# Modulation products kept whole on four column strips, and first squares added in pairs, in a decoder layer with product-key experts

## What is computed

```python
mod = silu(c) @ w_ada + b_ada        # c: 9 conditioning vectors of 1024, w_ada 1024 x 6144
sh1, sc1, gt1, sh2, sc2, gt2 = split(mod, 6)
h = rms_norm(x, g_pre1) * (1 + sc1) + sh1
P = h @ w_in                         # 3584 columns: q, k, v, g, and B, C, xv of a short convolution
m = concat(retention(q, k, v, g), short_conv(B, C, xv)) @ w_out
x = x + gt1 * rms_norm(m, g_post1)
h = rms_norm(x, g_pre2) * (1 + sc2) + sh2
x = x + gt2 * rms_norm(peer(h), g_post2)
```

## Time and profile before

| | us |
|---|---|
| median of 3 runs | 1785.98 (1785.57 to 1786.85) |
| the profiled execution | 1788.07 |
| its span, first to last instruction | 1786.3 |
| PE busy | 1737.2 (97%) |
| VectorE busy | 1095.5 (61%) |
| ScalarE busy | 587.0 (33%) |
| GpSimd busy | 1052.1 (59%) |
| mean granted TensorE clock | 0.991 of full |

### The profile page before, as it was taken

The page is one execution under the profiler, slowest core; times in us unless marked ns, Lnnn a source line. Parts: engine busy times, 40 slices in busy tenths (PEclk is TensorE's granted clock), DMA queues, the critical chain, the costliest instruction groups (busy, mean ns, idle before and its releaser), DMA issues.

```text
span 1786.3 us, 31229 instructions
## 1 busy us (share of the span) xinstructions
PE 1737.2 (97%) x12724; PEld 1695.1 (95%) x12724; DVE 1095.5 (61%) x2204; ACT 587.0 (33%) x764; POOL 1052.1 (59%) x693
## 2 busy tenths in 40 slices
PE   7989999999999999999999999999999999999996
PEld 5989979699999999999999999999999999999996
DVE  5624586567477456667562222225888989888884
ACT  5222264332233323232222222223333333333332
POOL 0330100006687888888888888873667787767631
PEclk9999999999999999999999999999999999999997
DMA  8523399673466665666657666668999999999971
GB/s 327 189 83 120 122 363 322 216 233 83 99 130 134 139 126 125 143 126 126 143 119 146 139 142 142 132 138 313 363 354 358 362 364 370 367 366 376 380 295 48
DMA packets 192358, 385.18 MB, mean 216 GB/s; under 512 B 74376, under 2 KB 132104, under 8 KB 177368
## 3 DMA queue, kind: packets, MB, share of 16 engines
q1 hardware_dynamic: 111864, 306.56, 50.5%
q0 software_dynamic: 80352, 76.65, 19.7%
HBM read 318.44 MB, written 64.19 MB: 214 GB/s over the span
## 4 chain that ended last, share of the span: by engine, by line
PE 51%; DVE 10%; issue 7%; POOL 3%; DMA 2%; ACT 0%; DVEq 0%; SPq 0%; ACTq 0%
PE ps L1672 27%; PE ps L1692 23%; DVE ul L1862 2%; DMA qp<-vtab,packed_choice 2%; POOL qp L1826 2%; POOL ag L1819 1%; DVE topi L135 1%; DVE top L129 1%; DVE topi L125 0%; PE ps L1649 0%; DVE h L214 0%; DVE h L223 0%; DVE h L228 0%; DVE pick L218 0%; DVE pick L235 0%
## 5 line engine op out<-in xcount | busy, mean ns | idle before, releaser
L100 POOL DMA_INDIRECT gates_dram<-gate,where x384 | 646.6, 1684 | 271.0 <-DVE where L251 130.9
L1672 PE MATMUL ps<-hl,uh 128*128 128x260 f32 x2048 | 414.3, 283 | 7.6 <-DVE ul L1862 7.6
L1672 PE MATMUL ps<-hh,ul 128*128 128x260 f32 x2048 | 414.0, 284 | 0.0
L1672 PE MATMUL ps<-hh,uh 128*128 128x260 f32 x2048 | 413.4, 284 | 0.0
L1862 DVE TENSOR_TENSOR ul<-us,uh 128x1024 fp32r<-128x1024 f32 x132 | 161.0, 1223 | 365.0 <-issue 280.4
L1692 PE MATMUL ps<-cl,uh 128*128 128x384 f32 (+1 forms) x1024 | 345.2, 337 | 3.2 <-DVE ul L1862 1.8
L1692 PE MATMUL ps<-ch,ul 128*128 128x384 f32 x1024 | 344.1, 336 | 0.0
L1692 PE MATMUL ps<-ch,uh 128*128 128x384 f32 x1024 | 344.1, 336 | 0.0
L1672 PEld LDWEIGHTS ps<-hl,uh 128*128 128x128 f32 x2048 | 317.0, 189 | 8.8 <-DVE ul L1862 8.6
L1672 PEld LDWEIGHTS ps<-hh,ul 128*128 128x128 f32 x2048 | 317.0, 189 | 0.0
L1672 PEld LDWEIGHTS ps<-hh,uh 128*128 128x128 f32 x2048 | 316.2, 189 | 0.0
(11 more groups left out here) (245 smaller groups left out, 2240.6 us busy)
## 6 DMA issues: line engine op xcount, KB each, us to landing
us<-utab SPq DMA_DIRECT2D x128, 512.0 KB
pairs<-vtab SPq DMA_DIRECT2D x62, 1024.0 KB
gates_dram<-blank SPq DMA_DIRECT2D x24, 1024.0 KB, 9.7
ahead_dram<-a SPq DMA_DIRECT2D x128, 192.0 KB
qp<-ahead_dram SPq DMA_DIRECT2D x32, 768.0 KB
gt<-gates_dram SPq DMA_DIRECT2D x32, 768.0 KB
wr<-w_ada SPq DMA_DIRECT2D x21, 1024.0 KB, 7.7
wr<-w_in SPq DMA_DIRECT2D x13, 1024.0 KB, 4.8
```

Source lines behind the costliest of these rows:

```text
L100: nc.gpsimd.indirect_dma_start(out=io["gates"].rearrange("g p c a t -> (g p c a t)").unsqueeze(1), out_offset=bass.IndirectOffsetOnAxis(ap ...
L1672: last = nc.tensor.matmul(out[:, half, :], w, r[:, k, half * TH:(half + 1) * TH], start=(k == 0 and q == 0), stop=(k == KD - 1 and q == 2))
```

## The change

Every modulation product is whole. `cs` is padded to 32 columns with zeros; the eight k-tiles go in turn to four column strips, that is to output partitions 0 to 31, 32 to 63, 64 to 95 and 96 to 127 of one PSUM bank, two k-tiles accumulating on each. ScalarE copies all 128 partitions, and the turn multiplies by `pick_row`, which adds the four partial rows. The split loads of w_ada, `cp`, `both` and the extra split buffers are gone, with their `high` and `low` calls in the start and in the heads. The first w_in load stands third in the order, no longer sixth. PE makes four products before the first blocks (product and turn three times, then a product) and the others ahead of k = 1 to 4. The squares of the first norm are added in pairs on VectorE, so that PE sums four tiles and not eight. The 24 clearing writes stand two behind each of the loads 11 to 22 (the projections), no longer behind the last 24.

The diff, cut to its core (buffers and semaphores that only vanish are left out):

```diff
@@ -52,6 +52,8 @@
+STRIP = 32
+STRIPS = P // STRIP
@@ -59,7 +61,7 @@
-    order = [(ADA, at) for at in shift_and_scale[:5]] + [(WIN, 0)] + [(ADA, at) for at in shift_and_scale[5:]]
+    order = [(ADA, at) for at in shift_and_scale[:2]] + [(WIN, 0)] + [(ADA, at) for at in shift_and_scale[2:]]
@@ -351,10 +349,10 @@
-        cs = sb(stack, "cs", [P, KD, 1 + NS])
-        cp = sb(stack, "cp", [P, KD, 2 * (1 + NS)], F32R)
-        rows = sb(stack, "rows", [2 * (1 + NS), 2, WC])
-        both = sb(stack, "both", [2 * (1 + NS), 1 + NS])
+        cs = sb(stack, "cs", [P, KD, STRIP])
+        rows = sb(stack, "rows", [P, 2, WC])
+        pick_row = sb(stack, "pick_row", [P, 1 + NS])
+        given = rows[:, 1, 0:KD * (1 + NS)].rearrange("p (k c) -> p k c", k=KD)
@@ -470,18 +461,13 @@
-        def is_split(row):
-            return row < ROWS_2 and row not in (0, 4)
...
-                if not is_split(n_rows - 1):
-                    continue
-                used.append((mod_mm, n_rows))
+                continue
@@ -506,7 +490,7 @@
-                sp.dma_start(cs[:], io["cT"]).then_inc(in_c, 16)
+                sp.dma_start(given, io["cT"]).then_inc(in_c, 16)
@@ -528,10 +512,10 @@
-                    c = n - len(order) + CLEARS
+                    c = 2 * (n - ROWS_1 - 3)
...
-                    if 0 <= c < CLEARS:
+                    for c in range(c, c + 2) if 0 <= c < CLEARS else ():
@@ -540,10 +524,9 @@
-                        sp.wait_ge(wl_ok, FIRST_IN + 1)
+                        sp.wait_ge(mod_mm, 5)
...
-                        sp.wait_ge(mod_mm, ROWS_1)
@@ -573,25 +556,19 @@
-                    return high_buffers[buffer_of(i)], low_buffers[buffer_of(i)]
+                    return wh[:, i % 2], wl[:, i % 2]
...
-                    out = ps[0:2 * (1 + NS), banks[n % len(banks)], 0:WC]
-                    if is_split(n):
-                        hi, lo = parts()
-                        for k in range(KD):
-                            for w in (hi, lo):
-                                last = nc.tensor.matmul(out, cp[:, k, :], w[:, k, :],
-                                                        start=(k == 0 and w is hi), stop=(k == KD - 1 and w is lo))
-                    else:
-                        w = raw_buffers[weights(n)]
-                        for k in range(KD):
-                            last = nc.tensor.matmul(out[0:1 + NS], cs[:, k, :], w[:, k, :],
-                                                    start=(k == 0), stop=(k == KD - 1))
+                    bank = banks[n % len(banks)]
+                    w = raw_buffers[weights(n)]
+                    for k in range(KD):
+                        strip = slice(k % STRIPS * STRIP, (k % STRIPS + 1) * STRIP)
+                        last = nc.tensor.matmul(ps[strip, bank, 0:WC], cs[:, k, :], w[:, k, :],
+                                                start=(k < STRIPS), stop=(k >= KD - STRIPS))
@@ -609,10 +586,7 @@
-                        if is_split(n):
-                            last = nc.tensor.matmul(turned, made_rows, both[:], start=True, stop=True)
-                        else:
-                            last = nc.tensor.transpose(turned, made_rows[0:1 + NS], ident[0:1 + NS, 0:1 + NS])
+                        last = nc.tensor.matmul(turned, made_rows, pick_row[:], start=True, stop=True)
@@ -715,24 +689,30 @@
-                for k in range(KD):
-                    norm_sums(k, sq_ok, 1 + k // 2)
-                pe.wait_ge(clo_ok, 1)
-                pe.wait_ge(both_ok, 1)
-                ada_product()
-                ada_turn()
-                ada_product()
+                for n in range(KD // 2):
+                    pe.wait_ge(added_ok, n + 1)
+                    for a in range(2):
+                        last = nc.tensor.matmul(pair(SUMS)[:, a, :], ones, mix[:, 2 * n, a * TH:(a + 1) * TH],
+                                                start=(n == 0), stop=(n == KD // 2 - 1))
+                last.then_inc(ss_mm, 1)
+                pe.wait_ge(silu_c, 1)
+                pe.wait_ge(pick_row_ok, 1)
...
+                ada_product()
...
-                    if k == 1:
-                        for _ in range(3):
-                            ada_product()
-                            ada_turn()
-                    if k == 2:
+                    if k in (1, 2):
+                        ada_turn()
+                        ada_product()
+                    if k == 3:
+                        ada_product()
+                        ada_turn()
+                    if k == 4:
+                        ada_product()
+                        ada_turn()
@@ -856,18 +836,16 @@
-                        some = slice(0, (2 if is_split(n) else 1) * (1 + NS))
-                        nc.scalar.activation(rows[some, n % 2, :], ps[some, banks[n % len(banks)], 0:WC], ACT.Copy)\
+                        nc.scalar.activation(rows[:, n % 2, :], ps[:, banks[n % len(banks)], 0:WC], ACT.Copy)\
...
-                    if i >= 4:
-                        act.wait_ge(*used[split_before.get(i, i - 2)])
-                    nc.scalar.activation(high_buffers[buffer_of(i)], raw_buffers[raw_slot(n)], ACT.Copy)\
-                        .then_inc(wh_ok, 1)
+                    if i >= 2:
+                        act.wait_ge(*used[i - 2])
+                    nc.scalar.activation(wh[:, i % 2], raw_buffers[raw_slot(n)], ACT.Copy).then_inc(wh_ok, 1)
@@ -898,43 +876,38 @@
-                nc.scalar.activation(cs[:], cs[:], ACT.Silu).then_inc(silu_c, 1)
-                act.wait_ge(silu_c, 1)
-                nc.scalar.activation(cp[:, :, 0:1 + NS], cs[:], ACT.Copy).then_inc(chi_ok, 1)
+                act.wait_ge(pad_ok, 1)
+                nc.scalar.activation(cs[:, :, 0:1 + NS], given, ACT.Silu).then_inc(silu_c, 1)
...
+                copy_rows(2)
                 high(0)
-                copy_rows(1)
-                high(1)
-                high(2)
-                copy_rows(2)
-                high(FIRST_IN)
...
+                high_prompt(0)
                 copy_rows(1)
-                high_prompt(0)
-                high(4)
                 high_prompt(1)
-                high(5)
                 copy_rows(1)
-                high(6)
                 high_samples(1)
+                copy_rows(1)
+                high_prompt(2)
+                high_prompt(3)
                 copy_rows(2)
-                high_prompt(2)
                 high_samples(2)
+                high_prompt(4)
                 copy_rows(1)
-                for k in (3, 4, 5):
-                    high_prompt(k)
+                high_prompt(5)
+                high(1)
                 high_samples(3)
-                for k in (6, 7):
-                    high_prompt(k)
+                high_prompt(6)
+                high_prompt(7)
...
-                    if i + 1 < N_IN:
-                        high(IN_AT + i + 1)
+                    if 1 < i + 1 < N_IN:
+                        high(i + 1)
@@ -952,10 +925,8 @@
-                high(HEADS_AT)
...
-                high(HEADS_AT + 1)
@@ -996,12 +966,12 @@
-                    high(HEADS_AT + 3 * hd + 3)
+                    if hd == RH - 1:
+                        high(OUT_AT)
...
-                        high(HEADS_AT + 3 * hd + 4)
@@ -1048,8 +1018,9 @@
+                nc.gpsimd.memset(cs[:], 0.0).then_inc(pad_ok, 1)
                 nc.gpsimd.memset(blank[:], 0.0).then_inc(blank_ok, 1)
-                pool.wait_ge(mod_mm, 5)
+                pool.wait_ge(mod_mm, 4)
@@ -1204,42 +1174,41 @@
-                dve.wait_ge(chi_ok, 1)
-                nc.vector.tensor_tensor(cp[:, :, 1 + NS:2 * (1 + NS)], cs[:], cp[:, :, 0:1 + NS].bitcast(F32),
-                                        ALU.subtract).then_inc(clo_ok, 1)
                 dve.wait_ge(in_cst, 16)
-                nc.vector.tensor_tensor(both[:], ident[0:2 * (1 + NS), 0:1 + NS],
-                                        ident[0:2 * (1 + NS), 1 + NS:2 * (1 + NS)], ALU.add).then_inc(both_ok, 1)
+                part = lambda n: ident[:, n * STRIP:n * STRIP + 1 + NS]
+                link(nc.vector.tensor_tensor(pick_row[:], part(0), part(1), ALU.add))
+                link(nc.vector.tensor_tensor(pick_row[:], pick_row[:], part(2), ALU.add))
+                nc.vector.tensor_tensor(pick_row[:], pick_row[:], part(3), ALU.add).then_inc(pick_row_ok, 1)
+                for n in range(KD // 2):
+                    dve.wait_ge(sq_ok, n + 1)
+                    nc.vector.tensor_tensor(mix[:, 2 * n], mix[:, 2 * n], mix[:, 2 * n + 1], ALU.add)\
+                        .then_inc(added_ok, 1)
                 inverse_rms(1)
-                for i in range(3):
-                    low(i)
...
+                low(0)
                 scaled_row(1)
-                low(FIRST_IN)
...
-                low(4)
+                low_prompt(1)
                 mod_pair(1)
-                low(5)
-                low(6)
                 scaled_row(2)
-                low_prompt(1)
...
```

(40 more changed lines are left out.)

## The result

The changed kernel took 1772.6 us (median of 4 runs, 1772.4 to 1776.2) against 1786.4 us before: a ratio of 0.9925, 95% interval 0.9911 to 0.9938, 13.8 us less. The forecast was 1770.4 us in a range of 1761 to 1793, faster with a chance of 0.63.

What follows compares the result with a forecast made beforehand. TensorE (PE) was taken as the bound, busy 97% of the span, with the start a chain over several engines. Gains 9 + 8.3 - 1.7 = 15.6 us took 1788.1 to 1772.5, then 1770.4 for the median; range 1761 to 1793.

Steps and rivals of the forecast that it cites:

- The price of a product: PE's time per modulation product: 1.0 us with four strips side by side, against 1.87 split or 3.62 whole; chance 0.48.
- The rival of two strips at a time: Matmuls start in order, so only two strips overlap: 2.03 us a product, 3.3 us gained, 1782.7 us; chance 0.25.
- The start: From 0 to 56.1 us: second load's blocks begin near 46.0 us, 10 us earlier; 9 us kept as gain.
- the step of the sums: In the start, the first norm's paired sums end at 13.3 us instead of 15.8, as PE has no backlog.
- one such stretch on the path less often than not: In the start, a 3.5 us half-clock stretch after PE idles costs 1.7 us; gain cut from 10 to 9 us.
- The heads: Head stage, 217.9 to 285.3 us: 10.4 us from twelve products plus 0.7 less 2.8, so 8.3 us gained.
- The waits taken back: In the heads, PE waits 0.6 us for copied rows in three heads, plus 1.0 us in the last: 2.8 us.
- The 0.7 us for PE's waits on low parts: In the heads, PE's waits for a low part ahead of products vanish with the splits: 0.7 us gained.
- Behind the output projection: Four cheaper products gain nothing; PE idles about 5 us twice, and a half-clock last projection loses 1.7 us.
- The rival of no overlap: Strips do not overlap: 3.62 us a product, together 26 us slower, 1812 us; chance 0.17.
- The point of balance: Product price at which gains and losses sum to zero: about 2.2 us.
- the chances, 0.48, 0.10 and a little under half of 0.25: Chance of faster: four strips side by side, work covered anyway, part of two at a time; 0.65, less allowance 0.63.

Runs made afterwards that it cites:

- same_strip_twice: Changed kernel with neighbouring parts paired on one strip (0 and 1 on the first, 2 and 3 on the second, and so on): 1772.9 us, ratio 0.9932 to before.
- filler_start: Changed kernel plus twelve matmuls without use, 8 and 4 behind turns 2 and 3 of the start: 1775.1 us, ratio 0.9941 to before.
- the fillers and the moved split together: Changed kernel with unused matmuls in the start and around the second norm's squares, and the second W_in load's split moved last: 1767.8 and 1768.6 us.
- two_strips: Changed kernel with the eight parts of a product alternating between two column strips instead of four: 1784.7 us, ratio 0.9995 to before.
- filler_norm: Changed kernel plus twenty matmuls without use in each of the two gaps around the second norm's squares: 1774.2 us, ratio 0.9932 to before.
- clears_late: Changed kernel with the 24 clearing writes back at their old place, one behind each of the last 24 loads: 1782.1 us, ratio 0.9982 to before.
- the moved split: Changed kernel with the split of the second W_in load moved behind the last modulated rows in the start: 1770.2 us, ratio 0.9910 to before.

## Why the prediction was right

**The price of a product** was the step on which all else hung: 1.0 us forecast, 1.00 measured. The rival of two strips at a time would have needed matmuls to start in order; windows of 50 ns show four starting at once. In the changed kernel four neighbouring instructions could do that in order; what the rival had wrong there is that the second record of one holds up the next. same_strip_twice settles the order itself: in order, its product would take 2.26 us, and it takes 1.02. The rule of the Trainium skill ("TensorE: Matmul & The Clock Gate", section The mechanism) that matmuls start and end in strict order does not hold across strips for these matmuls. Its section Measured speedup vs the span model gives 2.38 times for three strips; no run here has three, and from 3.58 us two give 1.9 times and four 3.6 times.

**The start** was forecast at 9 us. At the beginning of the heads it is 4.0 us in the profiled run and 4.7 in the mean of three traces. The order of steps was right: constants, load pace, low part, k = 6 at 43.1 forecast and 46.2 measured, held by the very split that the step names. The second load's blocks, forecast at 46.0 us, start at 50.7. (In the step of the sums 11.3 + 0.7 + 4 x 0.25 is 13.0 and not 13.3; 14.0 was measured, and nothing hung on it.) The main term that failed is the clock: "one such stretch on the path less often than not". There were two in the start, of 10 and of some 3.5 us, and the first slowed products 2 and 3 to 1.9 us each and k = 0 to nearly twice its 1.4 us; in the trace above another stood behind the wait before the v projection (at 0.66 from 87 to 90 us), a wait of 2.4 us that was there before and had no such stretch then. With most of the first stretch gone (filler_start) k = 6 starts at 44.0 us, 1.2 to 2.2 us sooner, so that stretch is about half of the 3.1 us by which k = 6 was late. With the fillers and the moved split together the heads begin 8.9 and 7.8 us earlier than before, near the 9 of the forecast.

**The heads** were forecast at 8.3 us; they gave 9.4. The gross 10.4 us is right (two_strips gives 10.3 by its price). The waits taken back were overestimated: 0.53 and 0.54 us in two heads (not in three, since the last head has the mean sums between) and 0.8 us for the squares behind the w_out split, 1.9 us in place of 2.8. The 0.7 us for PE's waits on low parts came back as forecast.

**Behind the output projection** the forecast was a loss of 1.7 us. It was 0.3 us up to the query projection. That starts 13.1 us earlier than before and the search 10.9, another 2.2 us lost, 1.8 in the projection and 0.4 as a longer change-over to the search. The mechanism, a gap of 5 us and half clock behind it, stood in the text; filler_norm, without the half clock there, has 28.4 us and 95.4 for the projection, against 28.7 and 97.1.

**The clearing writes** were costed at nothing where they went, which held. What the text did not price is what they would have cost where they were. Its sentence on them in the heads named DMA at 0.95 and drew no figure from it; clears_late shows 6.3 us in the heads and 8 to 10 in all. So of the forecast's 8.3 us there, 6.3 us hung on a move that stood in the sum at zero.

**The sum** is closer in the total than in its terms, and part of that is luck. The terms gave 15.6 us; up to the search the profiled runs differ by 4.0 + 9.4 - 0.3 - 2.2 = 10.9 us, 11.3 with the mean of three traces. The medians differ by 13.8 us, so 2.5 to 3 us of that agreement stand outside the stages that were forecast. One possible source is the second half of the search, which lasts 3.6 us more in the profile of before than in two of the three of the changed kernel; how long it lasted in the other runs of before no trace shows.

The rival of no overlap was priced at 26 us slower than before and would have been 32: the heads as forecast (+21), the start at +12 and not +6. The point of balance lies near X = 1.9 us, where two_strips is level, not at 2.2. In the chances, 0.48, 0.10 and a little under half of 0.25 come to 0.69 and not to 0.65.

## What to carry to other kernels

A matmul with few output columns can be cut into four column strips and summed later, and the strips overlapped in both orders of the instructions that were tried; in this kernel it beats a split into rounded parts that takes work on two more engines. Taking work from an engine that is not the bound gives nothing (two_strips' heads), and taking it from PE opens gaps, which cost twice, as waits and as half clock behind them: look at what ends the new gap before looking at the clock (here the moved split lowered the median by itself, the fillers did not). When a stage gets shorter, look at the transfers that just fitted into it: clears_late suggests that they no longer do, and there they showed as a wait of ScalarE for a load and of PE for ScalarE.

## What the runs showed of the hardware that was not expected

Four strips of the array take full-precision matmuls at the same time with little loss: 1.00 us where a quarter of 3.58 is 0.90. And an instruction that waits for its strip lets later ones pass to theirs (1.02 us in same_strip_twice). The stretches at half clock behind a gap differ from run to run of the same code: 13.6 to 20.4 us of them before the heads of the changed kernel, which began at 211.2 to 214.4 us.
